# Pooling groups of a two-branch encoder kernel taken in the order 3, 2, 1, 0

## What is computed

```python
h = rmsnorm(x, norm_g)                                 # 1024 channels
a, g_a, u, v, g_b, r_a, r_b = split(h @ w_in)          # 4608 columns
# branch A: trailing-window mean minus the row itself, window 2, 4, 8, 16 on the channel groups 0..3
pa = pool_mix(a, prev, pos0)                           # 4 groups of 128 channels
pa = einsum('blgc,gcd->blgd', pa, w_pool) * pool_scale
y_a = (silu(g_a) * pa) @ w_a
# branch B: u * (W_s layernorm(v) + b) in chunks of 128 positions
y_b = (silu(g_b) * spatial_gate(u, layernorm(v), w_s, b_s)) @ w_b
y = rmsnorm(x + (sigmoid(r_a) * y_a + sigmoid(r_b) * y_b) @ w_o, final_g)
```

## Time and profile before

| | |
|---|---|
| median of 3 executions | 841.17 us (840.46 to 893.07) |
| the profiled execution: time | 840.58 us |
| its span, slowest core (core 5), granted clock | 839.0 us, 0.990 |
| core 1 | 838.1 us, 0.990 |
| the other six cores | 835.6 to 836.9 us, 0.990 to 0.994 |
| TensorE busy | 803.9 us (96%) |
| VectorE busy | 496.7 us (59%) |
| ScalarE busy | 271.1 us (32%) |
| GpSimd busy | 110.2 us (13%) |

### The profile page before, as it was taken

The page is one execution under the profiler, slowest core; times in us unless marked ns, Lnnn a source line. Parts: engine busy times, 40 slices in busy tenths (PEclk is TensorE's granted clock), DMA queues, the critical chain, the costliest instruction groups (busy, mean ns, idle before and its releaser), DMA issues.

```text
span 839.0 us, 13040 instructions; the slowest of 8 cores (835.6 to 839.0 us)
## 1 busy us (share of the span) xinstructions
PE 803.9 (96%) x4032; PEld 389.4 (46%) x4032; DVE 496.7 (59%) x813; ACT 271.1 (32%) x454; POOL 110.2 (13%) x277
## 2 busy tenths in 40 slices
PE   5779899999999999999999999999999999999996
PEld 3536445844444444444444444444444444444442
DVE  3457734666654675568564765557555756466435
ACT  3232322334232424233333324143423423242322
POOL 2362000221011201020001101020002001110001
PEclk9979999999999999999999999999999999999999
DMA  8959980553013220404022401413040501320202
GB/s 193 191 82 178 170 208 1 89 222 142 1 38 114 100 101 15 137 29 173 1 56 95 170 33 26 126 74 127 5 132 22 196 1 38 113 101 1 102 1 100
DMA packets 50949, 77.74 MB, mean 93 GB/s; under 512 B 33257, under 2 KB 33385, under 8 KB 50626
## 3 DMA queue, kind: packets, MB, share of 16 engines
q1 hardware_dynamic: 46176, 63.07, 23.5%
q0 software_dynamic: 4560, 13.76, 10.2%
q10 hardware_dynamic: 146, 0.08, 0.1%
HBM read 64.82 MB, written 18.50 MB: 99 GB/s over the span
## 4 chain that ended last, share of the span: by engine, by line
PE 78%; DVE 10%; issue 4%; DMA 4%; ACT 1%; SPq 1%; POOL 1%; DVEq 0%; POOLq 0%; ACTq 0%
PE ps L353 62%; PE ps L539 14%; DVE tmp L438 6%; DMA Wo<-xh 4%; SPq L269 1%; DVE pa L445 1%; PE ps L494 1%; DVE fa L463 1%; ACT junk L555 1%; DVE carry L456 1%; DVE xr L551 1%; DVE tmp L427 0%; POOL stats L301 0%; DVEq L106 0%; ACT tmp L426 0%
## 5 line engine op out<-in xcount | busy, mean ns | idle before, releaser
L353 PE MATMUL ps<-hT,Win 128*128 128x512 bf16 (+1 forms) x2304 | 493.0, 368 | 0.0
L353 PEld LDWEIGHTS ps<-hT,Win 128*128 128x128 bf16 x2304 | 224.4, 98 | 237.8 <-issue 1.8
L526 DVE TENSOR_TENSOR tmp<-ps,tmp 128x512 f32<-128x512 f32 (+1 forms) x72 | 47.6, 662 | 141.7 <-PE ps L353 136.8
L299 POOL TENSOR_SCALAR stats<-stats 128x1 f32<-128x1 f32 (+1 forms) x103 | 21.3, 207 | 692.9 <-ACT junk L309 360.7
L539 PE MATMUL ps<-Wo,mg 128*128 128x512 bf16 x512 | 111.8, 379 | 0.0
L518 ACT ACTIVATE tmp<-ps 128x512 f32<-128x512 f32 (+1 forms) x72 | 41.3, 573 | 147.3 <-PE ps L353 136.5
L539 PEld LDWEIGHTS ps<-Wo,mg 128*128 128x128 bf16 x512 | 50.1, 98 | 60.2
L551 DVE TENSOR_TENSOR xr<-ps,xr 128x512 f32<-128x512 f32 x68 | 46.7, 689 | 45.5 <-PE ps L539 41.4
L353 PE MATMUL ps<-fa,Wa 128*128 128x512 bf16 x256 | 66.5, 383 | 0.3 <-DVE fa L463 0.3
L353 PE MATMUL ps<-s_bf,Wb 128*128 128x512 bf16 x256 | 66.2, 381 | 0.0
L438 DVE TENSOR_TENSOR tmp<-tmp 128x512 f32<-128x512 f32 (+9 forms) x90 | 60.2, 669 | 9.8 <-DVE tmp L438 0.5
(11 more groups left out here) (97 smaller groups left out, 509.1 us busy)
## 6 DMA issues: line engine op xcount, KB each, us to landing
xr<-xp SPq DMA_DIRECT2D x64, 512.0 KB, 6.8
yp<-xr SPq DMA_DIRECT2D x32, 512.0 KB, 2.7
Win<-w_in POOLq DMA_DIRECT2D x18, 512.0 KB, 15.8
Wo<-w_o POOLq DMA_DIRECT2D x2, 1024.0 KB, 38.5
xr<-xs SPq DMA_DIRECT2D x3, 512.0 KB, 8.2
Wa<-w_a POOLq DMA_DIRECT2D x4, 256.0 KB, 30.3
Wb<-w_b POOLq DMA_DIRECT2D x4, 256.0 KB, 31.6
ys<-xr SPq DMA_DIRECT2D x2, 512.0 KB, 3.0
```

What stands on the lines that cost most here:

```text
L353: ins = e.matmul(out=bank[:, 0:cols_n], lhsT=l, rhs=r, start=(i == 0), stop=(i == n - 1))
L526: S.add("dve", lambda e: e.tensor_tensor(out=sa[:, 0:T], in0=ya[:, 0:T], in1=sa[:, 0:T], op=ALU.mult), [kya, ksa], [ksa])
```

## The change

The pooling groups are taken from group 3 (four adds, 16 rows) down to group 0 (one add, 2 rows), in all tiles. The weight blocks of a and g_a for groups 2 and 3 are loaded ahead of those for groups 0 and 1; `Wp` keeps its place. Nothing is added or removed.

```diff
-        order = [C_GB, C_U, C_GB + 256, C_U + 256, C_A, C_GA, "Wp", C_A + 256, C_GA + 256]
+        order = [C_GB, C_U, C_GB + 256, C_U + 256, C_A + 256, C_GA + 256, "Wp", C_A, C_GA]
...
         def stage_A(ts):
             pend = []
-            for g in range(4):
+            for g in (3, 2, 1, 0):
                 for t in ts:
                     if t.first:
                         carry_in(g)
```

## The result

Six executions of the changed kernel have a median of 861.13 us (860.16 to 862.28). The kernel before, timed beside it, has 841.41; the ratio is 1.0237, 95% interval 1.0226 to 1.0247. The profiled execution took 862.28; its slowest core is core 1 with a span of 860.7, the others have 856.6 to 859.7, and the mean granted clock of the cores is 0.979 to 0.983 where it was 0.990 to 0.994. While e5 to e12 ran, nearly every execution of every kernel, the one before included, had some cores at a mean clock of about 0.957 and about 21 us later than the others, so for these runs the text gives spans of single cores with a mean clock of 0.97 or more. For the kernel before such spans have a median of 838.5 beside e5 to e8 (44 spans, 835.8 to 840.6) and of 838.7 beside e9 to e12 (62 spans, 835.3 to 840.4).

A forecast was written before the change was run, and what follows sets the result against it. TensorE, busy 96% of the span, was taken as the bound. In us: 839.0 - 1.3 + 10.9 + 1.0 + 1.4 = 851.0, 852.6 with 1.58 outside the span, 860 with 7.6 for the clock; range 853 to 866.

The forecast's parts named there:

- The steady tile: Stage A of tiles 3 to 8: first finish 2.28 late, later ones on time; +10.9 us.
- Why the last finish was 0.4 late before: Steady tile, fourth finish: VectorE begins late, then runs without a break until it is 0.4 late.
- Tile 2: Stage A of tile 2, no stores ahead: first finish 4.07 late, the others on time; +1.0 us.
- The pair: First pair of tiles, t0 and t1: waits of 6.0 against 4.6 before; +1.4 us.
- Edits at no cost: Weight block order, buffer rings and the SyncE and GpSimd queues: no cost, no wait for a DMA.
- The clock: TensorE falls to half clock behind some gaps: 4.5 falls on the slowest core, 1.7 each; +7.6 us.
- One sign: Whole execution: the spans of the cores should differ by multiples of 1.7 us.
- B: Same waits at the head of stage A, with 0 to 2 clock falls: 852.6 to 856.0 us; chance 0.27.
- C: The clock falls after every gap: 866.2 us; chance 0.15.
- D: Stage A: late waits are what counts, the early one doesn't arise; not slower, 829 us; chance 0.05.

The follow-up runs named there:

- e5: Changed kernel with the last store scaling of the tile before moved behind the first group's chain; median core span 847.5 us, profiled execution 850.4 us.
- e12: Kernel before with single-tile finishes issued two groups later and order 0, 1, 3, 2 in the first pair; median core span 832.5 us.
- e8: Kernel before with each single-tile finish issued two groups later instead of one; median core span 833.1 us, ratio 0.9962.
- e9: Kernel before with each single-tile finish issued two groups later instead of one, timed once more; median core span 833.2 us.
- e7: Changed kernel with each single-tile finish issued two groups later instead of one; median core span 834.1 us, ratio 0.9974.
- e6: Kernel before with the last store scaling of the tile before moved behind the first group's chain; median core span 838.9 us.
- e2: Kernel before with order 3, 2, 1, 0 in the first pair and the new weight block order only; 842.5 us, ratio 1.0005.
- e4: Changed kernel with the weight blocks loaded in the order of before; 863.6 us, ratio 1.0253.
- e3: Changed kernel with matmuls whose result is thrown away put into TensorE's gap before the first finish; 853.4 us, ratio 1.0134.
- e1: Kernel before with order 3, 2, 1, 0 in the seven single tiles only; 863.0 us, ratio 1.0244.
- e11: Kernel before with order 0, 3, 2, 1 in the single tiles; executions of 843.95 and 844.39 us, median core span 841.7 us.

## Why the prediction was right, point by point

**The steady tile: right.** 2.28 late at the first finish was forecast, 2.18 is measured, with none behind it. The term of +10.9 measured 10.5 (core 1): 13.1 in place of 13.7, less 2.6 in place of 2.8. e5 shows the cause, VectorE's late start, and e7 the cure. One reading of the forecast was off without effect on the sum: VectorE does not work until 290.56 but idles for a part of it, as the timeline above shows.

**Why the last finish was 0.4 late before: wrong, without effect on the sum.** I put it down to VectorE running without a break. e6 took that away and the 0.4 stayed: the chain cannot start before ScalarE's copy of a, and VectorE's scaling ends at nearly the same time. In the sum it stood as a measured number.

**Tile 2: +1.0 forecast.** On core 0 it is +1.0 without the fall of the clock (from the stage's start to the fourth finish 23.71, less 1.69, against 20.98). On the slowest core it is +3.7, of which the fall is 1.3; the rest is that the chain starts 8.21 after the stage. It waits for ScalarE's copy of a, which stands behind four norms of v (L392), and their statistics VectorE takes only after its last scaling L563 for the stores of t1. That one starts 1.14 before the stage on core 1 (190.54) and 2.80 before it on core 0 (187.36). Why it comes later on core 1, I haven't tested.

**The pair: +1.4 forecast, +1.5 measured** between cores without a fall (e2's core 7 against core 0 of before, from the stage's start to the second r_a group: 34.39 against 32.89). The slowest core of the kernel before had lost 1.3 by its fall in the pair, e2's slowest profiled core has none there, so the two nearly cancel and e2 is 0.05% over before. The median core span of e2 is 1.0 over that of the kernel before (839.5 and 838.5).

**Edits at no cost: right.** e4.

**The clock: 7.6 forecast, 7.7 to 8.7 measured** by e3. I had 4.5 falls at 1.7 on the slowest core; it had six, of which four in steady tiles at 1.69, one in tile 2 at 1.3, and one in the pair, which shortened the waits behind it from 1.62 to 0.45. The forecast without a fall was 852.6, e3 has 853.4. This was the uncertain term: without it the change would be 1.3% slower, not 2.4%.

That the size came out is in part luck. I started from 2 falls per core, by the two of eight cores in one execution, and raised it to 4.5 because the slowest core counts. The eight cores had 6, 6, 4, 4, 5, 4, 4 and 5, a mean of 4.75, so the rate was more than twice mine and the step to the slowest core less than I took. One execution is too little for such a rate: behind the same wait in the same pair, two, three and seven of eight cores fell (before, e1, e11). The price of 1.7 was right in the steady tiles, but not in tile 2, where it was 1.3 to 2.9.

One sign did not come: the spans of the cores don't differ by multiples of 1.7. Core 0 with six falls has 858.1, core 3 with four has 858.0; tile 2, the start-up and the pair, where a fall is mostly regained in the waits behind it, blur it.

**The rivals.** B (no or few falls) is e3's time; it did not come by itself, as no core had fewer than four falls. C is a fall in every gap. "TensorE: Matmul & The Clock Gate", section "HAM oscillation — how this bites in real kernels" of the Trainium skill, tells of a kernel with longer waits than these, whose clock falls anew in every iteration. The trace agrees that a recurring wait brings recurring falls, but not in every tile: core 1 fell in four of six. On single cores C does come, in all six steady tiles and tile 2: core 3 of e4, and cores 2, 3 and 7 of e1. Two of e4's executions, 865.1 and 865.5, are near its 866.2. D is excluded: the store scaling stands ahead of the chain on every core.

## What to carry to other kernels

Find the point of a stage where the engine that fills in is furthest behind, and put the shortest chain there; how long a chain may be is read from when its engine becomes free, not from how much work lies beside it. Or issue the consumer one group later: that made the order nearly irrelevant. Where a wait of about 2 us recurs on TensorE, count the clock too: here it was two fifths of the loss, and matmuls that do nothing useful won it back.

## What was unexpected of the hardware

After a wait of 2.02 us in a stream of matmuls the clock fell in some tiles and not in others of the same core (tiles 5 to 8, not 3 and 4, on core 1; 26 of 48 over all cores), and the falls come in runs. Behind waits of 0.7 to 1.7 (profiles of before, the change, e1, e2, e3, e5 and e11, all cores) the granted clock was 1.00 each time. A fall in a steady tile cost 1.69 us each time. A longer wait is no certain fall either: one of 3.93 in tile 2 cost nothing on core 1 of e5, where the other seven cores fell.
